# First two weight blocks and x loaded and split in pieces in turns; squares behind them in PSUM; first norms and rotations 16 products later

## The chip, the cores and the metric

The kernel runs on one core of a Trainium2 chip. The metric is the device time of one execution in microseconds (us), the median over runs. Engines are called as in the profile: PE (TensorE, matmuls), ACT (ScalarE), DVE (VectorE), POOL (GpSimd) and SP (SyncE, which here only issues DMAs).

## The reference

One layer of a streaming encoder on 512 tokens of width 2048, all float32. Cut to what matters here:

```python
xn = rms_norm(h, norm1_gain)                 # h = x, 512 x 2048
proj = xn @ w_in                             # 2048 x 8704
qa, ka = partial_rope(rms_norm(qa)), partial_rope(rms_norm(ka))
y_a = sliding_window_sink_attention(qa, ka, va, sinks)
y_b = chunked_relbias_attention(rms_norm(qb), rms_norm(kb), vb, rel_bias)
mixed = g_a * (y_a @ w_branch_a) + g_b * (y_b @ w_branch_b)
h = h + mixed @ w_out
h = h + peer_ffn(rms_norm(h))                # product-key experts, 16384 of them
```

## The kernel before

All activations lie transposed in SBUF: features on the 128 partitions, 512 tokens along a row. Every large product is streamed: a **block** of weights is 128 x 2048 (1 MB, 16 tiles of 128 x 128), and `stream` (L1497) multiplies it with 16 operand tiles of 128 x 512. To keep float32 accuracy, weights and activations are split into a rounded high part and the rest, and each tile takes three **products** (high x high, high x low, low x high), so a block is 48 products on PE. Blocks are numbered; block b uses the buffers `w_raw`, `w_hi`, `w_lo` of number b mod 2.

A block goes through four engines. SP loads it into `w_raw` (`load`, L310 to L316) once the previous block has been split. ACT rounds it to `w_hi` (`hi`, L409 to L415), which waits until PE has finished block b - 2. POOL subtracts to get `w_lo` (`split`, L344 to L349, one instruction of 2048 columns; block 0 is done by DVE at L914 instead). PE then starts block b (`lo_ready`, L1501). Each engine works strictly in the order of its own code.

At the start x (4 MB, `x_raw`) is loaded in four parts of four tiles, behind block 0 and, for the last part, behind block 1. ACT scales and rounds each tile to `xn_hi` (L489), DVE makes `xn_lo` (L922), and PE waits before every tile of block 0 for its `xn_lo`. The squares of x, for the RMS norm, are taken by ACT (L493) into a ring of four buffers and summed by DVE into `sq` (L929, L931), in between those tiles. `sum_features` (L1551) sums `sq` over the partitions with a matmul of ones; from it ACT and DVE make `rstd_x` and `eps_x`.

Blocks 0 and 1 are the two K tiles of attention A, block 2 the first Q tile, blocks 3 and 4 the V tiles. A K or Q tile t then passes, each step on another engine: ACT copies it out of PSUM (`take`) and squares it (`square`), PE sums the squares per head (`sum_heads`, L1525), DVE makes the mean (`mean_square`, L954), ACT takes Ln and Exp (`rsqrt_guess`, L426), DVE corrects and applies it (`normed`, L897, of five instructions at L890, L892, L894, L901 and L903, with a drain between each two), PE rotates (`rotate`, L1532), DVE finishes the rotation (`rope`, L905 to L910). V is scaled by DVE and turned by PE (`turn_v`, L1536). These small matmuls stand in PE's stream as "extras" after a given number of products: `sum_heads` after 8 and `rotate` after 42 of the next blocks.

Attention A then runs in seven pairs of heads. Pair n has four blocks (5 to 8 for the first), and its six attention steps stand in PE's stream at products 12, 45, 78, 111, 144, 177 of the pair's 192 (`with_steps`, L1599). On ACT the weight rounding of the next blocks stands between the parts of the softmax (`pair_a`, L525).

Later stages (attention B, the output projections, the experts) stream in the same way and are not touched.

Of the kernel before, what the change touches and what calls it, by code (L numbers as in the profile page):

```python
# [7 lines left out]
S = 512  # L8
# [98 lines left out]
def build(nc, x_t, w_stream, small, keys_t, rel_ext, consts, down_rows, up_rows, out):  # L107
    ctx = ExitStack()
    with ctx:
# [105 lines left out]
        s_x = [sem(f"x_in{k}") for k in range(4)]  # L215
# [51 lines left out]
        def raw_count(base, j, i, per=4):  # L267

            return 16 * ((base + j) // 2 + 1) + 8 * per * i
# [22 lines left out]
        @block.sync  # L292
        def _(sp):
            def load_x(k):
                sp.dma_start(x_raw[:, 2048 * k:2048 * (k + 1)], x_t[:, 2048 * k:2048 * (k + 1)]).then_inc(s_x[k], 16)

            sp.dma_start(raw[0][:, :], w_stream[0]).then_inc(raw_in[0], 16)
            load_x(0)
            load_x(1)
            load_x(2)  # L300
            sp.dma_start(raw[1][:, :], w_stream[1]).then_inc(raw_in[1], 16)
            load_x(3)
# [7 lines left out]
            def load(i):  # L310
                for s in range(2):

                    need(sp, hi_ready, 2 * i + s - 1)
                    need(sp, lo_ready, 2 * i + s - 1)
                    src = w_stream[2 * i + s] if isinstance(i, int) else w_stream[bass.ds(2 * i + s, 1)].rearrange("a p c -> (a p) c")
                    sp.dma_start(raw[s][:, :], src).then_inc(raw_in[s], 16)  # L316

            repeat(sp, B_DOWN // 2, load, 1)
# [24 lines left out]
        def _(pool):  # L343
            def split(i):  # L344
                for s in range(1 if isinstance(i, int) and i == 0 else 0, 2):
# [40 lines left out]
            pool.wait_ge(lo_ready, 1)  # L386
            split(0)
# [20 lines left out]
        def _(act):  # L408
# [106 lines left out]
            rsqrt_guess(2)  # L515
            take_v(0, va[0][:, :])
# [8 lines left out]
            def pair_a(i, n0):  # L525
# [359 lines left out]
        def _(v):  # L885
# [27 lines left out]
            v.wait_ge(hi_ready, 1)  # L913
            vec.tensor_tensor(wlo[0][:, :], raw[0][:, :], whi[0][:, :].bitcast(F32), ALU.subtract).then_inc(lo_ready, 1)  # L914


            v.wait_ge(s_cols, 16)
            for k in range(4):
                v.wait_ge(s_x[k], 16)
# [6 lines left out]
                for c in {0: range(4), 1: range(4, 8), 2: (), 3: range(8, CT)}[k]:  # L926
                    v.wait_ge(xsq, c + 1)
                    if c == 0:
                        vec.tensor_copy(sq[:, :], x_sq[0][:, :]).then_inc(sq_acc, 1)  # L929
                    else:  # L930
                        vec.tensor_tensor(sq[:, :], sq[:, :], x_sq[c % 4][:, :], ALU.add).then_inc(sq_acc, 1)  # L931
                    v.drain()
# [561 lines left out]
        def _(pe):  # L1494
            mm = nc.tensor.matmul

            def stream(b, s, tiles, extras=None, before=None, width=S):  # L1497
# [3 lines left out]
                pe.wait_ge(lo_ready, b + 1)  # L1501
# [107 lines left out]
            def pair_a(i, n0, G, more=()):  # L1609
# [274 lines left out]
```

## Time and profile before

| | |
|---|---|
| median of 3 runs | 3585.38 us (3585.33 to 3587.41) |
| the profiled execution's own time | 3585.94 us |
| its span in the profile | 3584.1 us |
| PE busy | 3540.5 us (99%) |
| DVE, ACT, POOL busy | 60%, 40%, 57% |
| mean granted TensorE clock | 0.997 |

The span is the time from the first to the last recorded instruction; the execution is 1.8 us longer. "Busy" is the share of the span in which an engine had an instruction running. PE's matmuls are pipelined: one product starts 0.23 us after the one before, though its row shows 0.39 us, so its rows overlap. All that the change edits runs in the first 145 us of the span.

### The profile page before, as it was taken

The page shows a single profiled execution, that of the slowest core. Times are in us where ns is not written, and L with a number is a line of the kernel's source. Part 1 is how long each engine was busy: PE and PEld are TensorE (multiplying, and loading weights), DVE is VectorE, ACT ScalarE, POOL GpSimd, SP SyncE. Part 2 cuts the span into 40 slices and gives each one's busy share as a digit, 9 for nine tenths or more (in the row PEclk, how much of TensorE's full clock was granted, in tenths as well). Part 3 has the DMA queues.
Part 4 walks back from the last instruction along what each step waited for, and adds up shares of the span by engine and source line. Part 5 has one row for each costly group of instructions (what it writes and reads, how often), then busy time and mean ns, then how long its engine had stood idle before and what let it go on. Part 6 is the DMA issues. An engine that isn't in the chain of part 4 may idle for free.

```text
span 3584.1 us, 50859 instructions
## 1 busy us (share of the span) xinstructions
PE 3540.5 (99%) x20069; PEld 3218.9 (90%) x20069; DVE 2136.7 (60%) x3752; ACT 1418.0 (40%) x1782; POOL 2025.9 (57%) x696
## 2 busy tenths in 40 slices
PE   7999999999999999999999999999999999999999
PEld 5777777777788888899999999999999999999999
DVE  6333344444685139896666666533577777777774
ACT  5544545555422223333444444333333333333332
POOL 2333333333344434477666666677777777777774
PEclk9999999999999999999999999999999999999999
DMA  3322222222334332388989888899999899999994
GB/s 153 139 101 98 96 95 88 97 82 94 120 141 184 110 116 94 126 309 325 357 324 353 322 337 332 347 346 377 360 361 357 348 348 357 363 358 354 354 353 156
DMA packets 181721, 871.95 MB, mean 243 GB/s; under 512 B 15520, under 2 KB 69024, under 8 KB 90400
## 3 DMA queue, kind: packets, MB, share of 16 engines
q1 hardware_dynamic: 59376, 399.48, 30.2%
q0 software_dynamic: 46224, 336.61, 23.7%
q10 hardware_dynamic: 75936, 133.28, 10.1%
q8 instruction: 130, 2.13, 0.2%
q14 instruction: 55, 0.45, 0.0%
HBM read 805.32 MB, written 69.21 MB: 244 GB/s over the span
## 4 chain that ended last, share of the span: by engine, by line
PE 62%; issue 22%; DVE 6%; POOL 5%; DMA 3%; ACT 1%; DVEq 0%; POOLq 0%; SPq 0%; ACTq 0%
PE ps L1514 59%; POOL w_lo L348 5%; DVE ps L1304 4%; PE ps L1744 2%; DMA expert_rows<-down_rows,idx 1%; DMA w_e_raw<-w_stream 1%; DVE h_dense L1434 1%; POOL w_e_lo L355 1%; DVE expert_rows L1291 0%; PE ps L1678 0%; DMA g_dram<-gate_buf 0%; DVE hn_lo L1134 0%; POOL expert_rows L383 0%; ACT w_e_hi L721 0%; DMA x_raw<-x_t 0%
## 5 line engine op out<-in xcount | busy, mean ns | idle before, releaser
L355 POOL TENSOR_TENSOR w_e_lo<-w_e_raw,w_e_hi 128x2048 fp32r<-128x2048 f32 x256 | 1183.5, 4624 | 521.9 <-ACT w_e_hi L721 520.3
L348 POOL TENSOR_TENSOR w_lo<-w_raw,w_hi 128x2048 fp32r<-128x2048 f32 x115 | 538.5, 4682 | 931.9 <-ACT w_hi L415 931.9
L1514 PE MATMUL ps<-sn_hi,w_e_hi 128*128 128x352 f32 x2048 | 669.5, 327 | 7.9 <-POOL w_e_lo L355 5.2
L1514 PE MATMUL ps<-act_hi,w_e_hi 128*128 128x352 f32 x2048 | 664.7, 325 | 5.3 <-DVE h_dense L1434 3.2
L1514 PE MATMUL ps<-act_lo,w_e_hi 128*128 128x352 f32 x2048 | 661.5, 323 | 0.0
L1514 PE MATMUL ps<-act_hi,w_e_lo 128*128 128x352 f32 x2048 | 661.4, 323 | 0.0
L1514 PE MATMUL ps<-sn_hi,w_e_lo 128*128 128x352 f32 x2048 | 661.0, 323 | 0.0
L1514 PE MATMUL ps<-sn_lo,w_e_hi 128*128 128x352 f32 x2048 | 658.7, 322 | 0.0
L721 ACT ACTIVATE w_e_hi<-w_e_raw 128x2048 fp32r<-128x2048 f32 x256 | 489.3, 1911 | 197.6 <-DMA w_e_raw<-w_stream 123.4
L1291 DVE SCALAR_TENSOR_TENSOR expert_rows<-expert_rows,ps 128x2048 f32<-128x2048 f32 x160 | 363.3, 2284 | 202.6 <-DMA expert_rows<-down_rows,idx 112.2
L1514 PE MATMUL ps<-xn_hi,w_hi 128*128 128x512 f32 x1088 | 447.2, 411 | 18.1 <-DVE xn_lo L922 18.0
L1434 DVE TENSOR_TENSOR h_dense<-ps,h_dense 128x352 f32<-128x352 f32 x512 | 265.2, 522 | 273.8 <-PE ps L1514 271.7
L1514 PE MATMUL ps<-xn_hi,w_lo 128*128 128x512 f32 x1088 | 427.3, 393 | 0.0
L1514 PE MATMUL ps<-xn_lo,w_hi 128*128 128x512 f32 x1088 | 426.4, 392 | 0.0
L1514 PEld LDWEIGHTS ps<-act_hi,w_e_hi 128*128 128x128 f32 x2048 | 385.6, 188 | 14.9 <-DVE h_dense L1434 14.9
L1514 PEld LDWEIGHTS ps<-sn_hi,w_e_hi 128*128 128x128 f32 x2048 | 385.9, 188 | 8.5 <-POOL w_e_lo L355 8.5
L1514 PEld LDWEIGHTS ps<-sn_hi,w_e_lo 128*128 128x128 f32 x2048 | 387.7, 189 | 0.0
L1514 PEld LDWEIGHTS ps<-sn_lo,w_e_hi 128*128 128x128 f32 x2048 | 386.6, 189 | 0.0
L1304 DVE SCALAR_TENSOR_TENSOR ps<-expert_rows,acts,ps 128x2048 f32<-128x2048 f32 x158 | 372.2, 2356 | 24.0 <-DMA expert_rows<-up_rows,idx_x 9.5
L1514 PEld LDWEIGHTS ps<-act_hi,w_e_lo 128*128 128x128 f32 x2048 | 385.7, 188 | 0.0
L1514 PEld LDWEIGHTS ps<-act_lo,w_e_hi 128*128 128x128 f32 x2048 | 385.3, 188 | 0.0
L415 ACT ACTIVATE w_hi<-w_raw 128x2048 fp32r<-128x2048 f32 x116 | 221.9, 1913 | 252.4 <-PE ps L1514 211.6
(257 smaller groups left out, 4850.5 us busy)
## 6 DMA issues: line engine op xcount, KB each, us to landing
w_e_raw<-w_stream SPq DMA_DIRECT2D x256, 1024.0 KB, 8.1
w_raw<-w_stream SPq DMA_DIRECT2D x116, 1024.0 KB, 4.8
gel_dram<-gel_all ACTq DMA_DIRECT2D x32, 704.0 KB, 9.5
g_dram<-gate_buf ACTq DMA_DIRECT2D x11, 2048.0 KB, 13.2
gel_in<-gel_dram ACTq DMA_DIRECT2D x32, 704.0 KB, 6.3
g_exp<-g_dram ACTq DMA_DIRECT2D x32, 704.0 KB, 14.5
gate_dram<-g_raw ACTq DMA_DIRECT2D x32, 256.0 KB, 2.0
g_in<-gate_dram ACTq DMA_DIRECT2D x16, 512.0 KB, 6.1
```

The source lines that it names most:

```text
L348: nc.gpsimd.tensor_tensor(wlo[s][:, :], raw[s][:, :], whi[s][:, :].bitcast(F32), ALU.subtract).then_inc(lo_ready, 1)
L355: nc.gpsimd.tensor_tensor(e_lo[j % 4][:, :], e_raw[j % 4][:, :], e_hi[j % 3][:, :].bitcast(F32), ALU.subtract).then_inc(lo_ready, 1)
L415: nc.scalar.activation(whi[s][:, :], raw[s][:, :], ACT.Copy).then_inc(hi_ready, 1)
L721: nc.scalar.activation(e_hi[j % 3][:, :], e_raw[j % 4][:, :], ACT.Copy).then_inc(hi_ready, 1)
L1291: vec.scalar_tensor_tensor(out=row, in0=row, scalar=1.0, in1=by_row, op0=ALU.mult, op1=ALU.mult, accum_out=acts[:, col:col + 1]).then_inc( ...
L1304: vec.scalar_tensor_tensor(out=by_row, in0=row, scalar=acts[:, col:col + 1], in1=by_row, op0=ALU.mult, op1=ALU.add).then_inc(row_used, 1)
L1434: vec.tensor_tensor(hf, ps[:, (CT * g + f + 2) % 3, 0:TD], hf, ALU.add).then_inc(acc_done, 1)
L1514: m = mm(ps[:, bank, 0:width], lhs[:, w], r, start=(n % (3 * per) == 0), stop=(n % (3 * per) == 3 * per - 1))
L1744: m = mm(ps[:, GB, KEYS * t:KEYS * (t + 1)], oh2[r][:, KEYS * t:KEYS * (t + 1)], g_oh[r][:, KEYS * t:KEYS * (t + 1)], start=True, stop=True)
```

## The change

1. The first two weight blocks and x come in pieces of four tiles, in turns: SP issues piece 0 of block 0, two parts of x, piece 1, and so on, then the four pieces of block 1. ACT rounds a piece of block 0 and then its four tiles of x, DVE makes the low parts in the same order (now of block 1 too, which POOL did), and PE waits for each piece of the weights.
2. The load of block 2 is issued as soon as block 0 is split, ahead of the constants; block 3 follows them.
3. All squares of x come behind block 1's pieces on ACT, four before and twelve behind the rounding of block 2. DVE keeps the running sum in a PSUM bank and writes only the last sum to `sq`.
4. `sum_features` moves from block 1 to block 2, after 12 products. Each `sum_heads` of the first three tiles moves from 8 to 24, each `rotate` from 42 of a block to 10 of the next, both turns of V likewise; those of the last tile are now in the first attention pair, whose six steps start at product 28 and stand 32 apart.
5. ACT rounds block 6 before it copies the first V.

```diff
@@ sync
+            def load_piece(b, k):
+                sp.dma_start(raw[b][:, 512 * k:512 * (k + 1)], w_stream[b][:, 512 * k:512 * (k + 1)]).then_inc(w_in[b][k], 16)
+            for k in range(4):
+                load_piece(0, k)
+                load_x(2 * k)
+                load_x(2 * k + 1)
+            for k in range(4):
+                load_piece(1, k)
...
+            sp.wait_ge(hi_ready, 1)
+            sp.wait_ge(lo_ready, 1)
+            sp.dma_start(raw[0][:, :], w_stream[2]).then_inc(raw_in[0], 16)
             sp.dma_start(cst[:, 0:512], consts[:, 0:512]).then_inc(s_const, 16)
...
+            sp.wait_ge(hi_ready, 2)
+            sp.wait_ge(lo_ready, 2)
+            sp.dma_start(raw[1][:, :], w_stream[3]).then_inc(raw_in[1], 16)
@@ scalar
             act.wait_ge(s_cols, 16)
             for k in range(4):
+                hi_piece(0, k)
                 for c in range(4 * k, 4 * k + 4):
+                    if c % 2 == 0:
+                        act.wait_ge(s_x[c // 2], 16)
                     nc.scalar.activation(xn_hi[:, S * c:S * (c + 1)], x_raw[:, S * c:S * (c + 1)], ACT.Identity,
                                          scale=cols[:, C_G1 + c:C_G1 + c + 1]).then_inc(xhi_ready, 1)
+            for k in range(4):
+                hi_piece(1, k)
+            for c in range(4):
+                square_x(c)
             take(0, 0, k_st[:, :])
             hi(B_PRE, 2)
+            for c in range(4, CT):
+                square_x(c)
+            act.wait_ge(s_const, 80)
             act.wait_ge(ss_mm, 1)
@@ vector
+            for k in range(4):
+                lo_piece(1, k)
+            sq_ps = ps[:, YB, :]
+            for c in range(CT):
+                v.wait_ge(xsq, c + 1)
+                if c == 0:
+                    vec.tensor_copy(sq_ps, x_sq[0][:, :]).then_inc(sq_acc, 1)
+                else:
+                    vec.tensor_tensor(sq_ps if c < CT - 1 else sq[:, :], sq_ps, x_sq[c % 4][:, :], ALU.add).then_inc(sq_acc, 1)
+                v.drain()
@@ tensor
             proj(0, 0, before=lambda c: (xlo_ready, c + 1))
-            pe.wait_ge(s_const, 80)
-            proj(1, 1, {30: [sum_features]})
-            proj(2, 0, {8: [lambda: sum_heads(0, [(eps_ready, 1)])], 42: [lambda: rotate(0, 0, k_st[:, :])]})
-            proj(3, 1, {8: [lambda: sum_heads(1, [(rope_done, 1)])], 42: [lambda: rotate(1, 1, q_at[:, :])]})
-            proj(4, 0, {8: [lambda: sum_heads(2, [(rope_done, 2)])], 42: [lambda: rotate(2, 2, q_st[:, :])],
-                        48: [lambda: turn_v(0, [(rope_done, 3)])]})
+            proj(1, 1)
+            proj(2, 0, {12: [sum_features], 24: [lambda: sum_heads(0, [(eps_ready, 1)])]})
+            proj(3, 1, {10: [lambda: rotate(0, 0, k_st[:, :])], 24: [lambda: sum_heads(1, [(rope_done, 1)])]})
+            proj(4, 0, {10: [lambda: rotate(1, 1, q_at[:, :])], 24: [lambda: sum_heads(2, [(rope_done, 2)])]})
...
+            pair_a(0, 1, 0, [(10, lambda: rotate(2, 2, q_st[:, :])), (16, lambda: turn_v(0, [(rope_done, 3)])),
+                             (36, lambda: turn_v(1, [(v_sb, 1)]))], 28, 32)
```

**ACT, the start of the program.** The names `w_hi_51`, `w_hi_52` are the two weight buffers (blocks 0 and 1), `x4` is four such instructions in a row. Before:

```order
L415 ACTIVATE w_hi_51<-w_raw_49 128x2048
L489 ACTIVATE xn_hi<-x_raw,cols 128x512 x4
L493 ACTIVATE x_sq_139<-x_raw 128x512
L493 ACTIVATE x_sq_140<-x_raw 128x512
L493 ACTIVATE x_sq_141<-x_raw 128x512
L493 ACTIVATE x_sq_142<-x_raw 128x512
L489 ACTIVATE xn_hi<-x_raw,cols 128x512 x4
```

and in the changed program, from the last piece of block 0 to the first squares behind block 2:

```order
L496 ACTIVATE w_hi_51<-w_raw_49 128x512
L509 ACTIVATE xn_hi<-x_raw,cols 128x512 x4
L496 ACTIVATE w_hi_52<-w_raw_50 128x512 x4
L501 ACTIVATE x_sq_139<-x_raw 128x512
L501 ACTIVATE x_sq_140<-x_raw 128x512
L501 ACTIVATE x_sq_141<-x_raw 128x512
L501 ACTIVATE x_sq_142<-x_raw 128x512
L430 ACTIVATE k_st<-ps 128x512
L425 ACTIVATE w_hi_51<-w_raw_49 128x2048
L501 ACTIVATE x_sq_139<-x_raw 128x512
```

The squares stood between the tiles of x and stand now behind both blocks; twelve of them stand behind the rounding of block 2.

**PE, the first rotation** (the matmul that reads `k_st`). `w_hi0`, `w_hi1` tell the blocks of even and odd number. Before, it stood six products ahead of the end of block 2:

```order
L1514 MATMUL ps<-xn_hi_60,w_lo0_53 128x512
L1534 MATMUL ps<-k_st_116,cst_55 128x512
L1514 MATMUL ps<-xn_hi_60,w_hi0_51 128x512
L1514 MATMUL ps<-xn_lo_61,w_hi0_51 128x512
L1514 MATMUL ps<-xn_hi_60,w_lo0_53 128x512
```

and in the changed program after ten products of block 3:

```order
L1551 MATMUL ps<-xn_hi_60,w_lo1_54 128x512
L1551 MATMUL ps<-xn_hi_60,w_hi1_52 128x512
L1571 MATMUL ps<-k_st_116,cst_55 128x512
L1551 MATMUL ps<-xn_lo_61,w_hi1_52 128x512
L1551 MATMUL ps<-xn_hi_60,w_lo1_54 128x512
```

It moved by 16 products, over the boundary to block 3, and so behind PE's wait for that block's weights.

## Rows read from the trace of the kernel before

**Rows 1.** The page, part 1: busy time and share of each engine.

```profile
PE 3540.5 (99%) x20069; PEld 3218.9 (90%) x20069; DVE 2136.7 (60%) x3752; ACT 1418.0 (40%) x1782; POOL 2025.9 (57%) x696
```

**Rows 2.** Stretches: busy us of PE, PEld, DVE, ACT, POOL; clock; DMA share; GB/s.

```profile
20.00:22.00 2.00, 0.00 (x0) 0.00 (x0) 2.00 (x1) 2.00 (x5) 2.00 (x1) 1.00 1.08 423
26.00:28.00 2.00, 1.46 (x4) 1.17 (x5) 2.00 (x4) 0.51 (x1) 0.00 (x0) 0.50 0.99 414
```

**Rows 3.** Timeline of PE: start us, duration us, instruction, [idle before <- releaser].

```profile
11.04 0.77 PE L1514 MATMUL ps<-xn_hi,w_hi 128*128 128x512 f32 x1 [11.04 <-DVE xn_lo L922]
...
16.54 0.50 PE L1514 MATMUL ps<-xn_hi,w_hi 128*128 128x512 f32 x1
...
26.54 0.79 PE L1514 MATMUL ps<-xn_hi,w_hi 128*128 128x512 f32 x1 [6.94 <-DVE xn_lo L922]
...
30.03 0.39 PE L1514 MATMUL ps<-xn_hi,w_lo 128*128 128x512 f32 x1
...
40.48 1.02 PE L1554 MATMUL ps<-sq,cst 128*128 128x512 f32 x2
...
56.27 1.12 PE L1534 MATMUL ps<-k_st,cst 128*128 128x512 f32 x2 [0.21 <-DVE k_st L903]
...
82.92 1.12 PE L1534 MATMUL ps<-q_st,cst 128*128 128x512 f32 x2 [0.57 <-DVE q_st L903]
...
86.19 0.66 PE L1542 MATMUL ps<-cst,v_raw 128*128 128x128 f32 x4 [0.77 <-DVE q_st L910]
...
143.02 0.49 PE L1577 MATMUL ps<-ka,q_at 64*128 64x128 f32 x4
```

**Rows 4.** DMA issues of the first 60 us: KB each, median us to landing.

```profile
w_raw<-w_stream SPq DMA_DIRECT2D x6, 1024.0 KB, 5.0
cols<-small ACTq DMA_DIRECT2D x1, 42.5 KB, 5.4
```

**Rows 5.** Timeline of ACT.

```profile
19.44 4.99 ACT L489 ACTIVATE xn_hi<-x_raw,cols 128x512 fp32r<-128x512 f32 x8
...
41.54 0.69 ACT L499 ACTIVATE rstd_x<-ps,cols 128x512 f32<-128x512 f32 x1 [3.20 <-PE ps L1554]
...
44.13 0.62 ACT L424 ACTIVATE sq<-k_st 128x512 f32<-128x512 f32 x1
...
46.16 1.91 ACT L415 ACTIVATE w_hi<-w_raw 128x2048 fp32r<-128x2048 f32 x1
```

**Rows 6.** Timelines of DVE and POOL in the first 60 us.

```profile
25.73 5.39 DVE L922 SCALAR_TENSOR_TENSOR xn_lo<-x_raw,cols,xn_hi 128x512 fp32r<-128x512 f32 x8 [0.16 <-issue]
...
48.15 4.64 POOL L348 TENSOR_TENSOR w_lo<-w_raw,w_hi 128x2048 fp32r<-128x2048 f32 x1 [6.45 <-ACT w_hi L415]
...
48.34 0.69 DVE L957 SCALAR_TENSOR_TENSOR var<-ps,eps_x 128x512 f32<-128x512 f32 x1 [5.39 <-PE ps L1530]
...
52.02 1.31 DVE L890 TENSOR_TENSOR newt<-rst 128x512 f32<-128x512 f32 x1 [2.99 <-ACT rst L431]
...
55.52 0.69 DVE L903 TENSOR_TENSOR k_st<-k_st,newt 128x512 f32<-128x512 f32 x1
...
58.80 0.69 DVE L910 TENSOR_TENSOR ka<-ka,rope_t 128x512 f32<-128x512 f32 x1
```

**Rows 7.** Timelines of DVE and POOL at two later places where they meet.

```profile
975.74 0.43 DVE L1105 TENSOR_SCALAR mix_hi<-m 128x512 fp32r<-128x512 f32 x1
975.86 4.77 POOL L348 TENSOR_TENSOR w_lo<-w_raw,w_hi 128x2048 fp32r<-128x2048 f32 x1 [4.94 <-ACT w_hi L415]
976.24 4.94 DVE L1107 TENSOR_TENSOR mix_lo<-m,mix_hi 128x512 fp32r<-128x512 f32 x1
...
1289.73 3.39 DVE L1134 SCALAR_TENSOR_TENSOR hn_lo<-h,cols,hn_hi 128x512 fp32r<-128x512 f32 x5
...
1291.52 6.07 POOL L348 TENSOR_TENSOR w_lo<-w_raw,w_hi 128x2048 fp32r<-128x2048 f32 x1 [6.23 <-ACT w_hi L415]
```

**Rows 8.** The page, part 5: a DVE addition that reads and writes PSUM.

```profile
L1304 DVE SCALAR_TENSOR_TENSOR ps<-expert_rows,acts,ps 128x2048 f32<-128x2048 f32 x158 | 372.2, 2356 | 24.0 <-DMA expert_rows<-up_rows,idx_x 9.5
```

More of the change, by code:

```diff
@@ L212, in build @@
         g_dram = nc.dram_tensor("g_dram", [GATE_GROUPS, P, KEYS * GT], F32).ap()
-        s_x = [sem(f"x_in{k}") for k in range(4)]
+        s_x = [sem(f"x_in{k}") for k in range(8)]
+        w_in = [[sem(f"w{b}_in{k}") for k in range(4)] for b in range(2)]
+        w_first_hi, w_first_lo = [sem(f"w{b}_hi_pieces") for b in range(2)], [sem(f"w{b}_lo_pieces") for b in range(2)]
         warm = sem("scratch_cleared")
@@ L267, in raw_count @@
         def raw_count(base, j, i, per=4):
-            return 16 * ((base + j) // 2 + 1) + 8 * per * i
+            return 16 * ((base + j) // 2) + 8 * per * i
         def used_after(item):
@@ L294, in load_x, with load @@
             def load_x(k):
[L295 to L302, printed above, removed]
+                sp.dma_start(x_raw[:, 1024 * k:1024 * (k + 1)], x_t[:, 1024 * k:1024 * (k + 1)]).then_inc(s_x[k], 16)
+            def load_piece(b, k):
[6 more added lines that the diff above has]
+                load_piece(1, k)
+            def load(i):
+                for s in range(2):
+                    need(sp, hi_ready, 2 * i + s - 1)
+                    need(sp, lo_ready, 2 * i + s - 1)
+                    src = w_stream[2 * i + s] if isinstance(i, int) else w_stream[bass.ds(2 * i + s, 1)].rearrange("a p c -> (a p) c")
+                    sp.dma_start(raw[s][:, :], src).then_inc(raw_in[s], 16)
+            sp.wait_ge(hi_ready, 1)
+            sp.wait_ge(lo_ready, 1)
+            sp.dma_start(raw[0][:, :], w_stream[2]).then_inc(raw_in[0], 16)
             sp.dma_start(cst[:, 0:512], consts[:, 0:512]).then_inc(s_const, 16)
@@ L308, in _ @@
             sp.dma_start(fold[:, :], consts[:, 1920:1920 + XT]).then_inc(fold_in, 16)
[L310 to L318, printed above, removed]
+            sp.wait_ge(hi_ready, 2)
+            sp.wait_ge(lo_ready, 2)
+            sp.dma_start(raw[1][:, :], w_stream[3]).then_inc(raw_in[1], 16)
+            repeat(sp, B_DOWN // 2, load, 2)
             def load_experts(j):
@@ L344, in split @@
             def split(i):
-                for s in range(1 if isinstance(i, int) and i == 0 else 0, 2):
+                for s in range(2):
                     pool.wait_ge(hi_ready, 2 * i + s + 1)
@@ L384, in gather @@
                                              bass.IndirectOffsetOnAxis(index, 0)).then_inc(row_in[slot], 16)
-            pool.wait_ge(lo_ready, 1)
-            split(0)
+            pool.wait_ge(lo_ready, 2)
             with pool.Fori(1, B_DOWN // 2) as i:
@@ L515, in _ @@
             rsqrt_guess(2)
+            hi(B_ATT_A, 1)
             take_v(0, va[0][:, :])
@@ L925, in _ @@
                                              op0=ALU.mult, op1=ALU.subtract).then_inc(xlo_ready, 1)
[L926 to L932, printed above, removed]
+            for k in range(4):
[5 more added lines that the diff above has]
+                    vec.tensor_copy(sq_ps, x_sq[0][:, :]).then_inc(sq_acc, 1)
+                else:
+                    vec.tensor_tensor(sq_ps if c < CT - 1 else sq[:, :], sq_ps, x_sq[c % 4][:, :], ALU.add).then_inc(sq_acc, 1)
+                v.drain()
             v.wait_ge(s_const, 80)
@@ L1495, in _, with stream @@
             mm = nc.tensor.matmul
-            def stream(b, s, tiles, extras=None, before=None, width=S):
+            def stream(b, s, tiles, extras=None, before=None, width=S, pieces=None):
                 experts = isinstance(b, int) and b >= B_DOWN
                 w_hi, w_lo = (e_hi[(b - B_DOWN) % 3], e_lo[(b - B_DOWN) % 4]) if experts else (whi[s], wlo[s])
-                pe.wait_ge(lo_ready, b + 1)
+                if not pieces:
+                    pe.wait_ge(lo_ready, b + 1)
                 extras = extras or {}
@@ L1508, in stream @@
                     for c in range(per):
+                        if pieces and c % 4 == 0:
+                            pe.wait_ge(*pieces(c // 4))
                         if before and k == 0:
@@ L1547, in proj @@
             def proj(b, s, extras=None, before=None):
-                stream(b, s, [(MAIN + s, (tile_out, b - 1), xn)], extras, before)
+                first = lambda k: (w_first_lo[b], k + 1) if k < 3 else (lo_ready, b + 1)
+                stream(b, s, [(MAIN + s, (tile_out, b - 1), xn)], extras, before,
+                       pieces=first if isinstance(b, int) and b < 2 else None)
             def sum_features():
+                pe.wait_ge(s_const, 80)
                 pe.wait_ge(sq_acc, CT)
@@ L1607, in with_steps, with pair_a @@
                     proj(b, s, extras)
-            def pair_a(i, n0, G, more=()):
+            def pair_a(i, n0, G, more=(), first=12, gap=33):
                 n, a = n0 + i, n0 - 1 + i
@@ L1613, in pair_a @@
                            [(78, lambda: sum_heads(2 + n, [(v_sb, 2), (rope_done, 2 + n)])),
-                            (165, lambda: rotate(2 + n, 2 + n, q_st[:, :])), *more], 12, 33)
-            pair_a(0, 1, 0, [(20, lambda: turn_v(1, [(v_sb, 1)]))])
+                            (165, lambda: rotate(2 + n, 2 + n, q_st[:, :])), *more], first, gap)
+            pair_a(0, 1, 0, [(10, lambda: rotate(2, 2, q_st[:, :])), (16, lambda: turn_v(0, [(rope_done, 3)])),
+                             (36, lambda: turn_v(1, [(v_sb, 1)]))], 28, 32)
             with pe.Fori(0, 3) as i:
```

29 lines of the change are left out of this document (17 added, 12 removed).

## The prediction

> **What bounds the kernel now.** I read the page first: PE is busy for 99% of the span [rows 1], so only a gap in PE's stream is worth anything, and what is won there is kept if no new gap eats it. Then PE's timeline [rows 3]. It starts at 11.04 us, stops after 24 products and goes on at 26.54, after 6.94 us of idle time that DVE's `xn_lo` ends. It is also slow at first: the twelve products from 11.04 to 16.54 take 0.46 us each, the eight from 26.54 to 30.03 take 0.44. In the second place the granted clock is 0.50 of 2.4 GHz [rows 2]; in the first the clock row shows nothing. From 30.03 to 40.48 there are 46 products, 0.227 us each: the full pace. From 40.48 on only short waits stand there, for DVE's norms and rotations.
>
> The yardstick is the first attention step of pair 2 (143.02 [rows 3]): product 444 of the stream, after which the two programs have the same order.
>
> **Part 1, the start.** ACT can begin when the gains `cols` are in: issued at 0.75, 5.4 us to landing [rows 4], so 6.15. It then does 16 tiles of 0.62 us (4.99/8 [rows 5]) and four pieces of about 0.6 (1.91/4 is the floor): done at 18.4. DVE follows from 6.7 with 16 tiles of 0.67 (5.39/8 [rows 6]) and four pieces of about the same: done at 20.1. Data: 423 GB/s [rows 2] bring a piece and two parts of x (1.3 MB) in 3.1 us. Landings of 4.1 to 15.9 us for block 0 and x and 18.4 for block 1 are ahead of ACT. PE starts at 8.1; I charge the slow start of the 12 products once more (5.5 us), then 36 x 0.227 = 8.2: block 0 ends at 21.8, DVE's last tile (20.1) being no hindrance.
>
> Block 1 adds 48 x 0.227 = 10.9, and 12 products of block 2 bring PE to the new place of `sum_features` at 35.4. Block 2's weights: its load is issued at 17.6 and lands at 22.7 (5.0 [rows 4]), ACT rounds it at 23.1 to 25.0, POOL is done at 29.6, before 32.7. The squares: DVE is free at 22.8 and needs 16 x (0.69 + 0.08 for the drain) = 12.3, so 35.1, just in time. That an addition with the sum in PSUM costs no more is bounded by `var<-ps`, 0.69 beside a running POOL instruction [rows 6], from above by 0.76, and by 2356 ns for four times the width in and out of PSUM [rows 8], 0.59 each, from below. I take 0.69; 0.76 would cost 1.1 us.
>
> So `sum_features` starts at 35.4 with 108 products done, where it started at 40.48 with 78 done. Lead: 5.1 + 30 x 0.227 = **11.9 us**.
>
> **Part 2, what the lead meets.** Call the start of `sum_features` t. Everything behind it is a chain through ACT, DVE and POOL whose pace the change leaves alone, while PE arrives sooner: 12 products after t instead of 26, and so on.
>
> (a) First head sums: ACT's square is ready at t + 4.27 (44.13 + 0.62 [rows 5] - 40.48), PE is there at t + 0.87 (the small matmul's cost in the stream) + 2.72 = t + 3.6. Wait 0.75, and 0.1 to restart.
>
> (b) Block 3: ACT copies K tile 1 and starts the rounding at t + 4.7, without the wait it had before, and ends at t + 6.6; POOL 4.6 more [rows 6], t + 11.3. PE ends block 2 at t + 10.7. Wait 0.6.
>
> (c) **First rotation, now at product 10 of block 3**, PE there at t + 13.6. The norm: ACT's Ln and Exp follow the rounding by 3.95 us (52.02 - 46.16 - 1.91), DVE starts at t + 10.55 and is held at L890 to the end of POOL's instruction (1.31 us for 0.67 [rows 6]); L903 would start 2.73 after POOL's end (55.52 - 52.79), at t + 14.0. But ACT, now late against PE, squares K tile 1 and finds block 2 already finished at t + 10.9: it rounds block 4 from t + 11.45 to 13.4, and POOL asks for its next subtraction at t + 13.4, while DVE is in L901. Rows 7 show what follows: POOL asks at 975.86 during L1105; after it there is only a drain of 0.07 us, yet POOL gets in, and L1107, with two SBUF inputs, takes 4.94 us for 0.69. The same here: L903 is held to t + 18.4 and ends at 19.0. PE waits 5.5, and 0.1. (Before, that subtraction came after the rotation.) A chain without drains keeps POOL out: 6.07 us at 1291.52 beside five L1134 [rows 7]; `normed` has drains. After such a wait the clock may fall as it did after 6.94 us; eight slow products cost 8 x 0.21 = 1.7. Bounds 0 and 2.8 (twelve products, as at the start); I take 1.5.
>
> (d) Block 4: the rotation's result reaches DVE for the two last steps of `rope` (before: 58.80 + 0.69 is 3.2 after 56.27). For K tile 2 POOL's subtraction for block 5 lies on them: from t + 33.8 to 38.4, `rope` ends at R = t + 39.8, and the head sums of Q wait for it from t + 37.5: 2.3, and 0.1.
>
> (e) First pair: block 4 ends at R + 6.5, ACT rounds block 6 at once (edit 5), POOL asks at R + 8.6, and so does L903 for Q. If POOL is first, rotation 3, which PE reaches at R + 8.7, waits 5.2; if DVE is first, the rotation waits 0.6 and `rope` behind POOL makes the first turn of V wait 4.1. I take 5.2, 0.1 and again 1.5 for the clock.
>
> Sum of (a) to (e): 0.85 + 0.6 + 7.1 + 2.4 + 6.8 = 17.75. Against it stand the waits of the old program in the same stretch: 0.37 twice (0.21 of idle [rows 3] and the 0.16 by which a product's 0.39 overhangs its pace; K tile 2 alike), 0.73, 0.93, and 0.3 of restarts: 2.7.
>
> Result: -11.9 + 17.75 - 2.7 = **+3.1 us**.
>
> The rest at nothing: the moved matmuls cost PE what they did. The steps of pair 1 start 16 products later; the rounding of block 7 behind the first of ACT's copies (product 60) needs 8.2 us to POOL's end, PE needs it at product 96, 10.8 us later, so 2.6 of cover (blocks 8 and 9: about 1.9 and 1.6); uncovered, one costs at most POOL's 4.6. SP's 16 issues of 0.5 us end at 8.8, ahead of the data.
>
> Profiled execution 3585.94 + 3.1 = 3589.0; from the median of 3585.38 it would be 3588.5. Forecast **3588.7**. What a measurement of this kernel can tell from no change is about 0.2%, 7.2 us.
>
> **The rivals.**
>
> *No meeting of POOL and DVE* (0.16). If L903 and the rotations slip through at (c), (d) and (e), there remain (a), (b), 0.7 at the rotation and 0.9 at the turn: 3.1 in place of 17.75, so -11.9 + 3.1 - 2.7 = -11.5, 3574. For it: POOL's request at (c) precedes L903 by 0.6 us only. Against it: both hang on the same ACT instructions, and all rows of POOL and DVE together look like rows 7.
>
> *Only (c) is missed* (0.14): its wait shrinks to 1.3 with a 1.1 behind it, no slow clock; the rest stays: -2, 3584.
>
> *Block 2 lands late* (slower, 0.06). Twelve squares are queued on ACT behind its rounding, and `sum_features`, both table loads and every later rounding behind these. The decisive point is 23.3 us: each us later moves t by one. Its load queues behind 16 others; if it took twice its 5.0 us, t is 4.4 later: +7.5, 3593; three times, 3598. Against it: the queue is nearly empty at 17.6.
>
> *Small transfers* (0.02). A load of 1 MB lands after 5.0 us [rows 4], of which 2.5 are its data at 423 GB/s [rows 2]. If every piece paid the other 2.5 us in turn, the twelve of block 0 and x would take 12 x 2.5 + 12.5 = 42 us, block 0 would end near 45 in place of 21.8, and the time would be +26, 3612. Against it: rows 2 show the 423 GB/s at 20 to 22 us, when constants of 0.06 to 0.26 MB are in flight. The page "DMA: Bandwidth & Descriptors" of the Trainium skill, sections "Anatomy of one DMA" and "Bandwidth", speaks for this rival: it gives a fixed part of about 2.0 us per DMA and asks for 1 MB or more in each. By its figure the estimate would be 36 us and 3606.
>
> **Numbers.** Forecast 0.62, within it 3585.5 (no slow clock) to 3593 (slow clock at its bound, dearer additions). The range 3578 to 3594 takes in the forecast, the case without (c) and half of the late block; outside are the case without any meeting (0.16), the small transfers and the slower half of the late block. Faster by over 0.2% is the first rival and little else: 0.17. Slower by over 0.2%: 0.08. Same: 0.75.
>
> **What the new profile would show.** PE from about 8 us without a gap to block 2; `sum_features` near 35.4; then PE idle 5 to 6 us before the first rotation, the row naming DVE's L903 (now L928), which itself lasts about 5 us beside a POOL instruction; a second such wait at the third rotation or the turn of V. Wrong: L928 lasting 0.69 us, or a gap before block 1.

## The result and the profile after

The changed kernel takes 3589.57 us (median of 22 runs, 3581.76 to 3593.68), the kernel before took 3583.68 us beside it (22 runs, 3580.24 to 3587.98). The ratio is 1.0015, with an interval of 1.0009 to 1.0022: slower by 0.15%, which is less than the 0.2% that the prediction set as its bound, though over this many runs it is not nothing. The forecast of +3.1 us was right in kind and too small: it is +5.9. That the time itself lies only 0.9 us from the forecast 3588.7 is partly luck, for the kernel before came out 1.7 us lower here than the 3585.38 us that the forecast started from.

The page of the changed kernel, its head and the line of part 1 (its time was 3593.01 us; [rows 1] is the line of before):

```profile
span 3591.2 us, 50985 instructions
...
PE 3546.1 (99%) x20069; PEld 3223.5 (90%) x20069; DVE 2139.2 (60%) x3759; ACT 1419.8 (40%) x1788; POOL 2021.7 (56%) x695
```

PE is busy for 5.6 us more with the same 20069 matmuls, so part of the loss is slower matmuls and not idle time. In the changed kernel the products are L1551, the feature sum L1594, the head sums L1567, the rotation L1571, the turn of V L1579. PE's timeline, to hold beside [rows 3]:

```profile
8.90 0.77 PE L1551 MATMUL ps<-xn_hi,w_hi 128*128 128x512 f32 x1 [8.90 <-DVE xn_lo L953]
...
36.34 1.10 PE L1594 MATMUL ps<-sq,cst 128*128 128x512 f32 x2 [0.52 <-DVE sq L965]
...
42.15 1.10 PE L1567 MATMUL ps<-sq,cst 128*128 128x512 f32 x2 [1.97 <-ACT sq L434]
...
49.02 0.50 PE L1551 MATMUL ps<-xn_hi,w_hi 128*128 128x512 f32 x1 [0.32 <-POOL w_lo L359]
...
56.58 2.08 PE L1571 MATMUL ps<-k_st,cst 128*128 128x512 f32 x2 [4.97 <-DVE k_st L928]
...
77.96 1.69 PE L1567 MATMUL ps<-sq,cst 128*128 128x512 f32 x2 [2.13 <-DVE ka L935]
...
94.18 0.66 PE L1579 MATMUL ps<-cst,v_raw 128*128 128x128 f32 x4 [3.48 <-DVE q_st L935]
...
148.91 0.49 PE L1615 MATMUL ps<-ka,q_at 64*128 64x128 f32 x4
```

The hole of 6.94 us in block 0 is gone and nothing stands between 8.90 and the feature sum. That sum starts 4.1 us sooner and with 30 products more behind it. Then come five waits, and product 444 (the yardstick) is at 148.91 where it was at 143.02: **+5.9 us**, all of what the medians show. Three of the waits name VectorE. Its timeline and GpSimd's, at the four places where they meet:

```profile
26.33 4.63 POOL L359 TENSOR_TENSOR w_lo<-w_raw,w_hi 128x2048 fp32r<-128x2048 f32 x1 [25.87 <-ACT w_hi L425]
26.80 8.62 DVE L965 TENSOR_TENSOR ps<-ps,x_sq 128x512 f32<-128x512 f32 x11 [0.71 <-ACT x_sq L501]
...
50.87 0.75 DVE L926 SCALAR_TENSOR_TENSOR k_st<-k_st,cols,rst 128x512 f32<-128x512 f32 x1
51.22 4.76 POOL L359 TENSOR_TENSOR w_lo<-w_raw,w_hi 128x2048 fp32r<-128x2048 f32 x1 [2.25 <-ACT w_hi L425]
51.70 4.83 DVE L928 TENSOR_TENSOR k_st<-k_st,newt 128x512 f32<-128x512 f32 x1
...
72.00 4.59 POOL L359 TENSOR_TENSOR w_lo<-w_raw,w_hi 128x2048 fp32r<-128x2048 f32 x1 [16.02 <-ACT w_hi L425]
73.25 3.88 DVE L933 TENSOR_TENSOR ka<-q_at,cos 128x512 f32<-128x512 f32 x1
...
86.55 0.69 DVE L928 TENSOR_TENSOR q_st<-q_st,newt 128x512 f32<-128x512 f32 x1
...
88.28 4.54 POOL L359 TENSOR_TENSOR w_lo<-w_raw,w_hi 128x2048 fp32r<-128x2048 f32 x1 [11.69 <-ACT w_hi L425]
...
89.95 3.41 DVE L933 TENSOR_TENSOR q_st<-q_st,cos 128x512 f32<-128x512 f32 x1
```

At 26.33 the additions of the squares run beside GpSimd's subtraction at 0.70 each. At 51.22 GpSimd asks while L926 runs, which still takes its usual 0.75 us; behind it is a gap of 0.08 us, and then L928 takes 4.83 us in place of 0.69, to the end of the subtraction: the same picture as in [rows 7]. That GpSimd gets in at that gap is read from these times; no row shows the moment. At 73.25 and 89.95 the cosine products of `rope` are held.

ScalarE's timeline shows a term that nobody had:

```profile
7.25 2.62 ACT L509 ACTIVATE xn_hi<-x_raw,cols 128x512 fp32r<-128x512 f32 x4 [1.31 <-DMA x_raw<-x_t]
...
37.52 1.28 ACT L522 ACT_TABLE_LOAD   x1 [3.82 <-PE ps L1594]
```

The load of the table for Ln comes behind the wait for the feature sum now, so its 1.28 us are on the path; in [rows 5] ACT went straight from that wait (3.20) into the Ln at 41.54, because the load had run ahead of it:

```profile
37.06 1.28 ACT L499 ACT_TABLE_LOAD   x1
```

Last, windows with the granted clock (columns as in [rows 2]):

```profile
50.00:60.00 10.00, 5.03 (x13) 3.05 (x13) 7.58 (x6) 2.42 (x2) 4.76 (x1) 0.72 0.58 197
...
70.00:80.00 10.00, 7.87 (x28) 5.23 (x27) 7.91 (x8) 3.21 (x3) 4.59 (x1) 0.92 0.21 68
...
90.00:100.00 10.00, 6.52 (x26) 4.58 (x25) 5.53 (x6) 1.08 (x2) 2.81 (x1) 0.83 0.30 105
```

Behind each of the three waits for VectorE a part of the products runs at 1.2 GHz, even behind the one of 2.13 us. The feature sum and the first head sums, with waits of 0.5 and 2.0 us, have none.

### The profile page after: what moved, and what is told of

Its sections match the earlier page's. It is cut to its first block, busy times and chain, and to the rows that moved or that the text cites. A ratio compares the mean times of both kernels' runs of the same rounds, so it can differ in the third digit from the quotient of the medians.

```text
span 3591.2 us, 50985 instructions
## 1 busy us (share of the span) xinstructions
PE 3546.1 (99%) x20069; PEld 3223.5 (90%) x20069; DVE 2139.2 (60%) x3759; ACT 1419.8 (40%) x1788; POOL 2021.7 (56%) x695
## 3 DMA queue, kind: packets, MB, share of 16 engines
q8 instruction: 130, 2.13, 0.2%
## 4 chain that ended last, share of the span: by engine, by line
PE 87%; DVE 8%; DMA 2%; ACT 1%; POOL 1%; issue 1%; DVEq 1%; SPq 0%; ACTq 0%
PE ps L1551 80%; DVE ps L1338 4%; PE ps L1783 2%; PE ps L1615 1%; PE ps L1633 1%; PE ps L1625 1%; DMA expert_rows<-down_rows,idx 1%; DVE h_dense L1468 1%; PE ps L1567 1%; POOL w_e_lo L366 1%; PE ps L1717 0%; DMA g_dram<-gate_buf 0%; DVE expert_rows L1325 0%; DVE hn_lo L1168 0%; DMA x_raw<-x_t 0%
## 5 line engine op out<-in xcount | busy, mean ns | idle before, releaser
L1551 PE MATMUL ps<-sn_hi,w_e_hi 128*128 128x352 f32 x2048 | 670.1, 327 | 7.5 <-POOL w_e_lo L366 4.8
L1551 PE MATMUL ps<-act_hi,w_e_hi 128*128 128x352 f32 x2048 | 664.8, 325 | 5.6 <-DVE h_dense L1468 3.7
L1551 PE MATMUL ps<-act_lo,w_e_hi 128*128 128x352 f32 x2048 | 661.7, 323 | 0.0
L1551 PE MATMUL ps<-sn_hi,w_e_lo 128*128 128x352 f32 x2048 | 661.5, 323 | 0.0
L1551 PE MATMUL ps<-act_hi,w_e_lo 128*128 128x352 f32 x2048 | 661.1, 323 | 0.0
L1551 PE MATMUL ps<-sn_lo,w_e_hi 128*128 128x352 f32 x2048 | 659.0, 322 | 0.0
L1551 PE MATMUL ps<-xn_hi,w_hi 128*128 128x512 f32 x1088 | 447.9, 412 | 9.2 <-DVE xn_lo L953 8.9
L1551 PE MATMUL ps<-xn_lo,w_hi 128*128 128x512 f32 x1088 | 429.1, 394 | 0.0
L1551 PE MATMUL ps<-xn_hi,w_lo 128*128 128x512 f32 x1088 | 427.1, 393 | 0.0
L1551 PEld LDWEIGHTS ps<-act_hi,w_e_hi 128*128 128x128 f32 x2048 | 385.3, 188 | 15.2 <-DVE h_dense L1468 15.2
L1551 PEld LDWEIGHTS ps<-sn_hi,w_e_hi 128*128 128x128 f32 x2048 | 386.3, 189 | 8.2 <-POOL w_e_lo L366 8.2
L1551 PEld LDWEIGHTS ps<-sn_hi,w_e_lo 128*128 128x128 f32 x2048 | 387.5, 189 | 0.0
L1551 PEld LDWEIGHTS ps<-sn_lo,w_e_hi 128*128 128x128 f32 x2048 | 387.5, 189 | 0.0
L1551 PEld LDWEIGHTS ps<-act_hi,w_e_lo 128*128 128x128 f32 x2048 | 385.9, 188 | 0.0
L1551 PEld LDWEIGHTS ps<-act_lo,w_e_hi 128*128 128x128 f32 x2048 | 385.3, 188 | 0.0
```

Of the source, the lines that this page charges most:

```text
L1551: m = mm(ps[:, bank, 0:width], lhs[:, w], r, start=(n % (3 * per) == 0), stop=(n % (3 * per) == 3 * per - 1))
```

## The experiments

All are edits of the changed kernel. The yardstick in each is product 444: 143.02 before, 148.91 after. The time of a single run can't separate them: from product 444 on, where all twelve profiled kernels do the same work, the rest of the span lasted from 3436.6 to 3444.3 us. The yardstick has a spread of its own: in the ten traces whose start has the same code as the change, the feature sum began at 35.86 to 36.34 us. So a difference of two yardsticks holds up to 0.5 us that the edit did not make, and every trace is of one execution. Where it matters, I also count product 444 from the feature sum of its own trace.

**e1: GpSimd waits for the ropes.** The subtractions of blocks 4, 5 and 6 wait for the rope of K tile 1, K tile 2 and the first Q (and GpSimd's loop is written out for these blocks).

```diff
                     pool.wait_ge(hi_ready, 2 * i + s + 1)
+                    if isinstance(i, int) and 2 * i + s in {4: 1, 5: 2, 6: 3}:
+                        pool.wait_ge(rope_done, {4: 1, 5: 2, 6: 3}[2 * i + s])
```

> The changed kernel, but POOL does not start the subtraction of block 4, 5, 6 before the rope of tile 1, 2, 3 is done on DVE. The yardstick is the start of product 444 (first attention step of pair 2): 143.02 us in the kernel before, 148.91 in the changed one. Theory (POOL's subtractions hold DVE's instructions with two SBUF inputs, and PE waits for these): L928 of the first norm lasts 0.7 us instead of 4.8, the wait before the first rotation falls from 5.1 to about 0.8, that before the third head sums from 2.3 to 0, that before the first turn of V from 3.6 to 0.9, the slow clock behind them goes (6 us); product 444 starts at 133.7, the time is about 9 us under the kernel before (ratio 0.9974). Rival (the chain through ACT and DVE is late by itself, POOL only happens to run then): the waits stay and POOL's later start adds to them, product 444 at 149 or later, ratio 1.0015 or more.

Measured: 3582.60 us (11 runs), a ratio of 0.9995 to the kernel before (0.9986 to 1.0004), and product 444 at 142.87. PE's timeline, then VectorE and GpSimd:

```profile
52.00 1.12 PE L1575 MATMUL ps<-k_st,cst 128*128 128x512 f32 x2 [0.84 <-DVE k_st L932]
...
68.05 5.08 POOL L361 TENSOR_TENSOR w_lo<-w_raw,w_hi 128x2048 fp32r<-128x2048 f32 x1 [8.09 <-DVE ka L939]
68.77 4.91 DVE L985 SCALAR_TENSOR_TENSOR newt<-newt,rstd_x 128x512 f32<-128x512 f32 x1
...
81.52 2.05 PE L1575 MATMUL ps<-q_st,cst 128*128 128x512 f32 x2 [3.87 <-DVE q_st L932]
...
91.51 0.55 PE L1619 MATMUL ps<-ka,q_at 64*128 64x128 f32 x4 [2.39 <-DVE q_at L1057]
```

The wait at the first rotation shrinks from 4.97 to 0.84 and the third head sums wait for nothing (2.13 in the change), as the theory has it: the loss there was GpSimd's subtraction. But 133.7 was missed by 9 us, and the ratio of 0.9974 with it. The subtraction moved behind the second rope now holds VectorE's reciprocal factor of x (`first_rstd`, L985, 4.91 us), and the third rotation waits 3.87 for what follows from it. The first attention step waits 2.39 besides; e8 and e6 come back to that. Moving the pass had moved the collision.

**e2: only block 4 waits.** The same edit with `{4: 1}`.

> Only block 4's subtraction waits for the first rope. Theory: the first wait falls from 5.1 to about 0.8 us and its slow clock (2.4) goes, the two later waits stay about as they are: product 444 at 142.2. Rival (chain late by itself): 149.

Measured: product 444 at 142.43 (3580.89 us, one run). PE:

```profile
52.29 1.13 PE L1575 MATMUL ps<-k_st,cst 128*128 128x512 f32 x2 [0.84 <-DVE k_st L932]
...
71.42 1.59 PE L1571 MATMUL ps<-sq,cst 128*128 128x512 f32 x2 [2.13 <-DVE ka L939]
```

One wait less and the others as in the change: the first collision alone costs 6.5 us (148.91 - 142.43; 6.3 counted from the feature sum), a wait of 4.1 more plus the slow products behind it. The waits on blocks 5 and 6 in e1 were worth nothing together.

**e3: the factor in PSUM.** `normed` keeps its Newton factor in a PSUM bank for the first three tiles. GpSimd's order is not touched.

```diff
+                factor = ps[:, SC, :] if isinstance(t, int) and t < 3 else newt
-                newton(var, rst, newt)
+                newton(var, rst, factor)
...
```

> The changed kernel with the correction factor of the first three norms in a PSUM bank, so that the last instruction of the norm (L928 there) has one SBUF input; POOL's program is untouched. Theory (it is the second SBUF input that is held): that instruction lasts 0.7 us although POOL's subtraction runs, the first rotation starts near 52.5 instead of 56.6, the rope's second instruction, with two SBUF inputs, is now held in its place to 56, and the second head sums wait about 1 us: product 444 near 143.2. Rival (any DVE instruction is held while POOL subtracts, or the norm waits for something else): the instruction still lasts about 4.8 us and product 444 stays at 149.

Measured: product 444 at 142.88 (3585.98 us, one run). GpSimd and VectorE:

```profile
50.77 5.11 POOL L359 TENSOR_TENSOR w_lo<-w_raw,w_hi 128x2048 fp32r<-128x2048 f32 x1 [2.27 <-ACT w_hi L425]
51.52 0.69 DVE L929 TENSOR_TENSOR k_st<-k_st,ps 128x512 f32<-128x512 f32 x1
...
54.04 2.39 DVE L934 TENSOR_TENSOR ka<-k_st,cos 128x512 f32<-128x512 f32 x1
```

GpSimd comes in at the same point of the chain, yet the product with one input in PSUM takes 0.69 us; the next instruction with two SBUF inputs is held to the end of the subtraction. So it is not being beside GpSimd that costs, but two inputs in SBUF. The Trainium skill says this on its page "SBUF — State Buffer", section "SBUF: two separate sides": a VectorE instruction with two SBUF inputs and a GpSimd instruction that reads SBUF take a shared pair of ports in turns, each for its whole length. The rows agree, with 4.83 us in the change against 0.69 here.

**e4: the table load.** ScalarE's wait for the constants is dropped; the gains that it needs are waited for earlier.

```diff
-            act.wait_ge(s_const, 80)
             act.wait_ge(ss_mm, 1)
```

> The changed kernel without ACT's wait for the constants ahead of the Ln of the first norm (PE has waited for them already), so that the table load no longer stands behind the wait for the feature sum. Theory (the 1.3 us by which the first head sums came later than forecast are this table load): it ends before 36.3, Ln starts 1.1 us after the feature sum, the wait before the first head sums falls from 2.1 to 0.8 us, the rest moves along: product 444 at 147.6. Rival (the table load is hidden or the later wait takes it back): product 444 at 148.9.

Measured: product 444 at 147.22 (3593.33 us, one run). ACT, then PE:

```profile
33.67 1.28 ACT L521 ACT_TABLE_LOAD   x1
...
40.77 1.10 PE L1566 MATMUL ps<-sq,cst 128*128 128x512 f32 x2 [0.65 <-ACT sq L434]
```

With one wait ahead of the Ln, its table is loaded at 33.67, while ACT would idle; with the two waits of the change standing together the load came behind them, at 37.52. The other traces go the same way: the load ran ahead of the wait in all five with one wait there (before, e4, e6, e9, e10), and behind it in all seven with two. PE's wait falls from 1.97 to 0.65 and the yardstick comes 1.7 us sooner, 1.3 of it from the table load. On "ScalarE: Activation LUTs", section "What ACT_TABLE_LOAD costs", the Trainium skill adds about 1.4 us of draining to the load's 1.28. No row here shows that part: ACT starts the Ln at 38.81, just behind the load.

**e5: the sum of squares in SBUF.**

```diff
-            sq_ps = ps[:, YB, :]
+            sq_ps = sq[:, :]
```

> The changed kernel with one difference: the running sum of the squares stands in SBUF instead of PSUM, so that each of VectorE's additions has two inputs in SBUF. Theory (such additions are held by GpSimd's subtraction of block 2 until it ends at about 31, while additions with one input in PSUM run beside it): the additions begin at about 31 instead of 26.8, the feature sum starts at about 40.5 instead of 36.3, and product 444 at about 153 (152 to 155 with the clock after a wait of 5 us). Rival (the additions run beside the subtraction wherever their operands stand): the feature sum at 36.3 and product 444 at 148.9.

Measured: product 444 at 152.82 (3592.38 us, one run). GpSimd, VectorE, PE:

```profile
26.29 4.61 POOL L359 TENSOR_TENSOR w_lo<-w_raw,w_hi 128x2048 fp32r<-128x2048 f32 x1 [25.83 <-ACT w_hi L425]
...
26.76 13.31 DVE L965 TENSOR_TENSOR sq<-sq,x_sq 128x512 f32<-128x512 f32 x12 [1.00 <-ACT x_sq L501]
...
40.22 1.12 PE L1594 MATMUL ps<-sq,cst 128*128 128x512 f32 x2 [4.42 <-DVE sq L965]
```

Twelve additions take 13.31 us here, where eleven took 8.62 with the sum in PSUM. The feature sum is 3.9 us later and so is the yardstick. The choice of PSUM is worth 3.9 us, which the prediction had in its sum by taking 0.69 for each.

**e8: e1, and the reciprocal factors ahead.** `first_rstd` goes ahead of `mean_square(0)`, where VectorE waits for the head sums anyway.

```diff
+            first_rstd()
             mean_square(0)
...
-            first_rstd()
             mean_square(2)
```

> The changed kernel with GpSimd's subtractions of blocks 4, 5 and 6 each waiting for the rope before, and VectorE's three first reciprocal factors computed ahead of the first mean square. Theory (with the waits alone the third rotation was late by 3.9 us because GpSimd's next pass, started right behind the second rope, held VectorE's reciprocal factors for 4.9 us): that wait goes, and product 444 starts at 134 to 137, against 142.9 with the waits alone. Rival (the third rotation is late for another reason, such as the chain of norm and rope itself): product 444 stays within 1 us of 142.9.

Measured: product 444 at 138.15 (3581.73 us, one run), 4.7 less than in e1, with no wait at the third rotation: the cause named in e1 holds for that wait. It is 1 us beyond the expected range, for a wait left at the first attention step:

```profile
86.79 0.53 PE L1619 MATMUL ps<-ka,q_at 64*128 64x128 f32 x4 [2.38 <-DVE q_at L1057]
```

**e6: e8 and e4 together.**

> The changed kernel with the GpSimd waits, the reciprocal factors moved ahead, and ScalarE's table load freed of its redundant wait. Theory (these three hold all of the loss but the clock's): product 444 at 132.5 to 135, 8 to 10 us ahead of the kernel before, so a time of 3573 to 3576 and a ratio of .997 to .998 against it. Rival (what is gained in the first 150 us is given back later, since the transfers of the rest are late by then): product 444 early, but the ratio at .999 or above.

Measured: 3577.48 us (11 runs), ratio 0.9982 (0.9973 to 0.9991), product 444 at 136.92. That is 6 us ahead of the kernel before in both measures, so nothing of it is given back later. The 132.5 to 135 were missed by 2, and the 3573 to 3576 by 1.5, at the same place as in e8:

```profile
79.80 4.58 POOL L361 TENSOR_TENSOR w_lo<-w_raw,w_hi 128x2048 fp32r<-128x2048 f32 x1 [8.10 <-DVE q_st L938]
...
81.53 3.41 DVE L1001 TENSOR_TENSOR v_raw<-v_raw,rstd_x 128x512 f32<-128x512 f32 x1 [1.87 <-ACT v_raw L434]
...
85.51 0.49 PE L1618 MATMUL ps<-ka,q_at 64*128 64x128 f32 x4 [2.37 <-DVE q_at L1056]
```

It is the same collision once more, now with the scaling of the values.

**e9: e6, and block 6 waits for the values.**

```diff
                         pool.wait_ge(rope_done, {4: 1, 5: 2, 6: 3}[2 * i + s])
+                        if 2 * i + s == 6:
+                            pool.wait_ge(v_scaled, 2)
```

> The kernel with the three edits (waits of GpSimd, factors ahead, table load), and GpSimd's subtraction of block 6 now also waits until VectorE has scaled the second tile of values. Theory (the wait of 2.4 us left at the first attention step comes from VectorE's scaling of the values, 3.41 us instead of 0.69 under that subtraction): the scaling takes 0.7, no wait at the first attention step, the granted clock stays up behind it, and product 444 starts at 133 to 135 against 136.9; time 3573 to 3577. Rival (the query's copy for the first step is late for another reason, or the later subtraction makes block 6 late): product 444 stays at 136.5 or later.

Measured: **3572.78 us** (6 runs, 3570.63 to 3577.99; before 3585.12 beside it), ratio 0.9968 (0.9956 to 0.9980), product 444 at 132.46:

```profile
81.12 0.69 DVE L1003 TENSOR_TENSOR v_raw<-v_raw,rstd_x 128x512 f32<-128x512 f32 x1 [1.86 <-ACT v_raw L436]
...
81.99 4.81 POOL L363 TENSOR_TENSOR w_lo<-w_raw,w_hi 128x2048 fp32r<-128x2048 f32 x1 [10.68 <-DVE v_raw L1003]
...
132.46 0.49 PE L1620 MATMUL ps<-ka,q_at 64*128 64x128 f32 x4
```

The yardstick came 4.5 us sooner. Of these, 0.4 were there before the edit can act (first head sums at 40.37, in e6 at 40.73), so a wait of 2.37 us taken away brought 4.1: the products behind it ran at 2.4 GHz again. This version is 12.3 us ahead of the kernel before, beside which it ran. The changed kernel did not run beside it; in its own comparison that one was 5.9 us behind the kernel before.

**e7: the old places.** Loads, squares, feature sum and first head sums as in the change; rotations behind product 42 of blocks 2, 3 and 4 as before, with the other head sums, the turns of V and ScalarE's order.

```diff
-            proj(2, 0, {12: [sum_features], 24: [...]})
-            proj(3, 1, {10: [... rotate(0, ...)], 24: [...]})
+            proj(2, 0, {12: [sum_features], 24: [...], 42: [... rotate(0, ...)]})
+            proj(3, 1, {8: [...], 42: [... rotate(1, ...)]})
...
```

> The changed kernel with the new loads, squares, feature sum and first head sums kept, but the rotations and the other head sums at the places of the kernel before (rotations behind product 42 of blocks 2, 3 and 4). Theory (the shift by 16 products is what put GpSimd's subtraction of block 4 between norm and rope): no wait of 5 us at the first rotation, the rhythm of the kernel before from there, and product 444 at 138 to 142. Rival (the shift itself gains, as its idea is, and the losses lie elsewhere): product 444 at 149 or later.

Measured: 3580.49 us (10 runs), ratio 0.9992 (0.9983 to 1.0001), product 444 at 140.41. VectorE, then PE:

```profile
51.31 0.69 DVE L926 TENSOR_TENSOR k_st<-k_st,newt 128x512 f32<-128x512 f32 x1
...
52.06 1.63 PE L1569 MATMUL ps<-k_st,cst 128*128 128x512 f32 x2 [3.48 <-DVE k_st L926]
...
140.41 0.49 PE L1614 MATMUL ps<-ka,q_at 64*128 64x128 f32 x4
```

With the start as in the change, the shift by 16 products, with all that moved along with it, costs 8.5 us (148.91 - 140.41; 8.1 counted from the feature sum). At the old places GpSimd's subtraction of block 4 does not fall on the norm: L926 takes 0.69 us. PE waits 3.48 here for another reason: it arrives before the first norm is made, which is what the shift is for.

**e10: e7 and e4.**

> The kernel with the rotations at their places of before (products 42), now also with ScalarE's table load freed of its redundant wait. It asks whether the shift by 16 products is worth anything once its collisions are gone (the kernel with the shift and all four edits has product 444 at 132.5). Theory (the shift gives TensorE work while norm and rope of the first tile are made): with the old places the wait at the first rotation stays, at about 2.2 us of its 3.5, and product 444 starts at 137.5 to 139.5, against 140.4 with the table load as in the change. Rival (the shift gives nothing of its own): no wait over 1 us at the first rotation, and product 444 at 133 to 135.

Measured: 3580.59 us (10 runs), ratio 0.9990 (0.9980 to 0.9999), product 444 at 139.63. PE:

```profile
50.77 2.07 PE L1568 MATMUL ps<-k_st,cst 128*128 128x512 f32 x2 [5.05 <-DVE k_st L925]
```

The rotation comes 1.3 us sooner than in e7, but the wait there grew where I had it shrink: PE was let through at the head sums and arrives the sooner. The expected range was just missed. The rival falls: against e9 the old places cost 7.2 us. But e9 has two kinds of edit more (GpSimd's waits and the factors ahead), so not all of that is shown to be the shift's.

## Why the prediction was right, and where it was short

**The start held, 0.9 short.** The lead was to be 11.9 us and was 10.95: 40.48 - 36.34, and 30 products at 0.227. Windows of the first transfers, of the changed kernel:

```profile
2.00:4.00 2.00, 0.00 (x0) 0.00 (x0) 0.00 (x0) 0.69 (x2) 0.00 (x0) 1.00 0.78 169
...
6.00:8.00 2.00, 0.00 (x0) 0.00 (x0) 0.69 (x1) 0.75 (x2) 0.00 (x0) 1.00 1.01 372
```

and of the kernel before, which starts with transfers of 1 MB:

```profile
2.00:4.00 2.00, 0.00 (x0) 0.00 (x0) 0.00 (x0) 0.69 (x2) 0.00 (x0) 1.00 0.82 284
...
6.00:8.00 2.00, 0.00 (x0) 0.00 (x0) 0.06 (x1) 1.91 (x1) 0.00 (x0) 1.00 0.99 418
```

I had let the data flow at 423 GB/s at once. The pieces start slower than that, and slower than the whole blocks did; the first part of x reached ACT at 7.2, after 1.31 us of idle time, and PE began at 8.90 instead of 8.1. Half a microsecond of that came back, since the first twelve products took 4.98 us and I had charged 5.5. Then the additions waited 0.71 at 26.80 for the squares behind ACT's rounding of block 2, where I had counted VectorE's 16 steps without a gap; that chain ended at 36.2 instead of 35.1, and PE, ready for the feature sum at about 35.7, waited for it. Additions at 0.69 beside GpSimd were right (e5 shows the other case). The rival of the small transfers is dead: block 0 was done near 22 us and not 45. What the rows show of a price for the pieces is the slower start.

**The steps behind the lead**, each measured as the delay it puts into PE's stream up to product 444:

| step | predicted | measured | from |
|---|---|---|---|
| lead | -11.9 | -10.95 | feature sum at 36.34 |
| (a) first head sums | 0.85 | 2.2 | 42.15 - 36.34 - 3.59 |
| (b) block 3's weights | 0.6 | 0.5 | 0.32 and restart |
| (c) first rotation | 7.1 | 7.5 | 4.97, restart, clock 2.4 |
| (d) third head sums | 2.4 | 4.0 | 2.13, restart, clock 1.75 |
| (e) first pair | 6.8 | 5.4 | 3.48, restart, clock 1.75 |
| waits of before | -2.7 | -2.7 | not measured anew |
| sum | +3.1 | +5.95 | trace: 5.89 |

(a) was mis-sized (0.85, which by its own terms, 4.27 - 3.6 and 0.1, should read 0.77; 2.2 measured) because I had not seen the table load: ACT's square was to be ready at t + 4.27, read off a trace in which the load had been done before the wait. The change puts the wait for the constants next to the one for the feature sum, and the load behind both; e4 gives it back. (c), the step that the whole forecast rested on, happened as written: GpSimd's request during L926, its way in at the drain, L928 at 4.83 us. The margin on which it hung was 0.6 us in the forecast and 0.48 in the trace. Counted from the feature sum GpSimd's request came 1.5 us later than I had it and L928 1.4 later: both hang on ACT, whose late table load moved them together. In e4, without that load on the path, they stand at 13.55 and 14.03 behind the feature sum, where the forecast had 13.4 and 14.0. e2 takes it away with the predicted effect, and e3 shows the mechanism without touching GpSimd. (d) had its wait right (2.3 said, 2.13 measured) and its clock wrong: I charged slow products only behind 5 us waits, and they come behind 2.13 too. (e) went the other of its two ways: VectorE was first at the norm (86.55), so the rotation did not wait and the turn of V did, 3.48 where I had 4.1. Its total was too large because I took the dearer way.

**The rivals.** Without any meeting of the two engines I had 3574 and 0.16. It did not happen, but e9, in which the meetings are arranged away, gives 3572.8, about what that case was worth. The rival that only (c) is missed is out by the row of L928 (its -2 should read about -1.5 by the terms given; its 3584 stands). Block 2's weights were there before PE needed them.

**What I had not foreseen** was how the collisions shift. For e1 I expected 133.7 from the forecast's own sum and got 142.87. It took e8 and e9 to find the two instructions (L985 in e1, L1001 in e6) that the moved subtractions hit next. Two things stay open. No run takes the drains out of `normed`, so that they are what lets GpSimd in is a reading of the rows, not a tested cause. And it is open which part of the 7.2 us between e10 and e9 is the shift alone.

## What to carry to other kernels

A step moved forward meets the other engines at another point of their chains. Before moving it, write down when each long GpSimd instruction starts and which VectorE instructions with two SBUF inputs lie in its length; either order them by a wait placed where VectorE is idle (e9), or give one input a place in PSUM (e3). After moving a pass, look for the next instruction in its way before calling the gain. Look for the table load when an activation has two waits standing together ahead of it. Price a wait of TensorE of over 2 us in such a stream at its length and about 2 us more: 1.7 (e6 to e9) to 2.4 (the first rotation) here, and nothing in one case (e3).

## What the runs showed of the hardware

- The granted clock fell behind short waits of TensorE, but not always. The twelve traces have 21 waits of over 2 us between the first product and product 444, and slow products followed 20 of them. Behind a wait of 2.13 us, products ran at 1.2 GHz in the change, e2, e4 and e5 (head sums of 1.69, 1.59, 2.08 and 1.81 us). In e3, after the same 2.13 us, the head sums took 1.12 us, as at 2.4 GHz. Behind the first head sums' wait of 1.95 to 1.99 us they took 1.10 us in the change, e1, e2 and e3, and 1.35 and 1.52 in e8 and e7.
- GpSimd does not need a long pause of VectorE to get in: it came in at gaps of 0.08 us, between instructions with a drain between them, in `normed` and `first_rstd` (51.62 to 51.70 in the change, 68.69 to 68.77 in e1), and the VectorE instruction behind it then took 4.8 to 4.9 us.
- The first transfers sped up step by step, and pieces of 0.25 and 0.5 MB more slowly than blocks of 1 MB: 169 GB/s at 2 to 4 us and 372 at 6 to 8, against 284 and 418.
